# Gate weights: the low halves beside the high halves in one stationary tile

## What is computed

```python
x = x + 0.5 * _swiglu(_rmsnorm(x, ffn1_norm), ffn1_w_gate, ffn1_w_up, ffn1_w_down)
h = _rmsnorm(x, mix_norm)
p = h @ w_in                     # 1024 x 3080
bg, cg, xin, q, k, v, o, ip, fp = jnp.split(p, offs, axis=-1)
li = ip + b_igate                # 4 heads
lf = jax.nn.log_sigmoid(fp + b_fgate)   # 4 heads
```

## Time and profile before

| | |
|---|---|
| median of 3 runs | 2062.49 us (2058.13 to 2064.17) |
| the profiled execution | 2062.03 us |
| its span | 2060.1 us |
| TensorE busy (matmuls) | 2002.5 us, 97%, 12520 matmuls |
| VectorE busy | 910.5 us, 44% |
| ScalarE busy | 503.3 us, 24% |
| GpSimd busy | 91.5 us, 4% |
| mean granted TensorE clock | 0.99 |
| chain that ended last | TensorE 91%, VectorE 5% |

### The profile page before, as it was taken

The page is one execution under the profiler, slowest core; times in us unless marked ns, Lnnn a source line. Parts: engine busy times, 40 slices in busy tenths (PEclk is TensorE's granted clock), DMA queues, the critical chain, the costliest instruction groups (busy, mean ns, idle before and its releaser), DMA issues.

```text
span 2060.1 us, 31004 instructions
## 1 busy us (share of the span) xinstructions
PE 2002.5 (97%) x12520; PEld 1984.1 (96%) x12520; DVE 910.5 (44%) x1563; ACT 503.3 (24%) x896; POOL 91.5 (4%) x145
## 2 busy tenths in 40 slices
PE   6999999999999998999999889999999999999998
PEld 6999999999999998999999889999999999999998
DVE  6523433333333338522677737533333333333334
ACT  5302111121121124343444423221111211121122
POOL 1000000000000013200000011100000000000001
PEclk9999999999999999999999999999999999999999
DMA  6012101110111011211112230121011101110102
GB/s 208 21 42 61 61 20 41 61 61 20 41 61 61 11 42 65 75 50 33 32 31 80 68 86 21 41 62 61 20 41 61 61 20 41 61 61 20 51 1 85
DMA packets 144177, 105.09 MB, mean 51 GB/s; under 512 B 6376, under 2 KB 136248, under 8 KB 144120
## 3 DMA queue, kind: packets, MB, share of 16 engines
q1 hardware_dynamic: 143992, 104.26, 16.5%
q10 hardware_dynamic: 128, 0.03, 0.0%
HBM read 95.36 MB, written 8.92 MB: 51 GB/s over the span
## 4 chain that ended last, share of the span: by engine, by line
PE 91%; DVE 5%; ACT 1%; DMA 1%; issue 1%; SPq 1%; ACTq 0%; DVEq 0%; POOL 0%
PE bank L204 29%; PE bank L210 28%; PE bank L209 28%; PE bank L208 1%; PE bank L206 1%; DVE ffn_normed L171 1%; DVE in_lo L163 1%; DMA raw<-in_w_out 1%; DVE ffn_root_work L143 0%; PE bank L1975 0%; PE bank L637 0%; PE bank L1989 0%; PE bank L1988 0%; PE bank L861 0%; DMA vector_rows<-in_cache_conv 0%
## 5 line engine op out<-in xcount | busy, mean ns | idle before, releaser
L204 PE MATMUL bank<-in_hi,w_hi 128*128 128x352 f32 x2256 | 738.8, 327 | 16.5 <-DVE in_lo L1128 7.5
L210 PE MATMUL bank<-in_hi,w_lo 128*128 128x352 f32 x2256 | 728.8, 323 | 0.0
L209 PE MATMUL bank<-in_lo,w_hi 128*128 128x352 f32 x2256 | 727.2, 322 | 0.0
L204 PEld LDWEIGHTS bank<-in_hi,w_hi 128*128 128x128 f32 x2256 | 425.8, 189 | 21.6 <-DVE in_lo L1128 8.1
L209 PEld LDWEIGHTS bank<-in_lo,w_hi 128*128 128x128 f32 x2256 | 428.0, 190 | 1.1
L210 PEld LDWEIGHTS bank<-in_hi,w_lo 128*128 128x128 f32 x2256 | 426.2, 189 | 0.0
L394 DVE TENSOR_TENSOR ffn_hidden<-ffn_silu,bank 128x352 f32<-128x352 f32 x132 | 68.8, 521 | 669.4 <-PE bank L210 579.6
L204 PE MATMUL bank<-ffn_hidden_hi,ffn_w_hi_more 128*128 128x352 f32 x1056 | 342.2, 324 | 0.9 <-ACT ffn_hidden_hi L341 0.8
L405 DVE SCALAR_TENSOR_TENSOR x<-bank,x 128x352 f32<-128x352 f32 x528 | 267.3, 524 | 159.5 <-PE bank L210 111.2
L210 PE MATMUL bank<-ffn_hidden_hi,ffn_w_lo_more 128*128 128x352 f32 x924 | 297.9, 322 | 0.0
L209 PE MATMUL bank<-ffn_hidden_lo,ffn_w_hi_more 128*128 128x352 f32 x924 | 297.6, 322 | 0.0
(11 more groups left out here) (227 smaller groups left out, 1500.6 us busy)
## 6 DMA issues: line engine op xcount, KB each, us to landing
raw<-in_ffn_w_gate SPq DMA_DIRECT2D x44, 512.0 KB, 3.9
ffn_raw_more<-in_ffn_w_down SPq DMA_DIRECT2D x44, 512.0 KB, 5.5
raw<-in_w_in SPq DMA_DIRECT2D x24, 512.0 KB, 3.9
raw<-in_ffn_w_up SPq DMA_DIRECT2D x22, 512.0 KB, 5.0
ffn_raw_more<-in_ffn_w_up SPq DMA_DIRECT2D x22, 512.0 KB, 5.3
x_parked<-x SPq DMA_DIRECT2D x3, 1408.0 KB, 5.6
x<-x_parked SPq DMA_DIRECT2D x3, 1408.0 KB, 9.9
raw<-in_w_out SPq DMA_DIRECT2D x8, 512.0 KB, 4.0
```

The source lines that it names most:

```text
L204: pe.matmul(out, w_hi, in_hi, start=first, stop=False)
L209: pe.matmul(out, w_hi, in_lo, start=False, stop=False)
L210: return pe.matmul(out, w_lo, in_hi, start=False, stop=last)
```

## The change

The gates' tile uses 8 of 128 stationary columns. In it the low halves of the gate weights now stand in columns 64 to 67 and 96 to 99 of the *high* tile of slot 0, beside the high halves in 0 to 3 and 32 to 35. One matmul with the high input gives both the high and the low weights' products, and one with the low input as well. So each feature step of the gates has two matmuls instead of three, 48 instead of 72 over the three blocks (and the product of low weight with low input, which was left out, is now in). The two output groups land on partitions 0 and 32 (high) and 64 and 96 (low) of the same bank, and VectorE adds them: six copies out of the banks into the row `m_`, and two adds of 1056 tokens. The numbers of the steps after it, waited for by ScalarE, VectorE and TensorE, rise by two.

```diff
+    def gates_low(dve):
+        dve.wait_ge(m.w_high, 1)
+        halves = sh.w_hi[0].rearrange("p (k e n) -> p k e n", k=KT, e=2)
+        raw = sh.raw[0].rearrange("p (k e n) -> p k e n", k=KT, e=2)
+        dve.tensor_tensor(halves[:, :, 1, :], raw[:, :, 0, :], halves[:, :, 0, :].bitcast(FP32), ALU.subtract
+                          ).then_inc(m.w_low, 1)
+
     def early_low(dve):
-        low(dve, 0, 0)
+        gates_low(dve)
         low(dve, 1, 1)
...
             row = rows[0:HEADS, ROW_M, 0:TOKENS]
-            act.wait_ge(s.row_step, 3)
+            act.wait_ge(s.row_step, 5)
             act.activation(row, row, ACT.Exp, scale=-1.0).then_inc(s.row_exp, 1)
...
             for which, dst in ((0, a), (1, wk)):
                 part = slice(32 * which, 32 * which + HEADS)
+                low_part = slice(64 + 32 * which, 64 + 32 * which + HEADS)
                 for b in range(BLOCKS):
-                    last = dve.tensor_scalar(dst[:, block_columns(b)], first_banks[2][b][part, 0:BLK],
-                                             gate_bias[part, :], None, ALU.add)
+                    dve.tensor_scalar(dst[:, block_columns(b)], first_banks[2][b][part, 0:BLK],
+                                      gate_bias[part, :], None, ALU.add)
+                    last = dve.tensor_copy(m_[:, block_columns(b)], first_banks[2][b][low_part, 0:BLK])
                 row(last)
+                row(dve.tensor_tensor(dst, dst, m_, ALU.add))
             row(dve.scalar_tensor_tensor(m_, wk, -1.0, wk, ALU.mult, ALU.max))
             low(2, 3)
...
                 pe.wait_ge(m.w_low, 1)
-                product(b, 2, first_banks[2][b])
+                for k in range(KT):
+                    col = slice(k * P, (k + 1) * P)
+                    for half in (sh.in_hi, sh.in_lo):
+                        last = pe.matmul(first_banks[2][b][:, 0:BLK], sh.w_hi[0][:, col], half[:, k, block_columns(b)],
+                                         start=k == 0 and half is sh.in_hi, stop=k == KT - 1 and half is sh.in_lo)
+                last.then_inc(s.dense_done, 1)
                 pe.wait_ge(m.w_low, 2)
```

More of the change, by code:

```diff
@@ L1436, in _ @@
             act.wait_ge(s.constants, CONSTANTS)
-            act.wait_ge(s.row_step, 20)
+            act.wait_ge(s.row_step, 22)
             for dst, src, scale in ((row_inter[:, :], row_inter[:, :], 1.0),
@@ L1448, in _ @@
             for i, rest in enumerate(both):
-                act.wait_ge(s.row_step, 21 + i)
+                act.wait_ge(s.row_step, 23 + i)
                 act.activation(middle_rows[i], rest, ACT.Copy).then_inc(s.row_exp, 1)
@@ L1631, in _ @@
             row(dve.tensor_tensor(decay_row[:, :], max_before[:, :], max_last[:, :], ALU.subtract))
-            assert step == 20
+            assert step == 22
             low(2, 6)
@@ L1644, in _ @@
                 dve.wait_ge(s.row_exp, 9 + 2 * i)
-                dve.wait_ge(s.row_step, 21 + i)
+                dve.wait_ge(s.row_step, 23 + i)
                 dve.tensor_tensor(row_parts[64:64 + HEADS, i, :], rest, middle_rows[i].bitcast(FP32), ALU.subtract
@@ L2066, in mixer_phase @@
         sh.norm = next_norm
-ROW_STEPS = 24
+ROW_STEPS = 26
 def out_phase(nc, sh, o, f):
```

## The result

| | before | after |
|---|---|---|
| median of 8 runs | 2063.85 us (2058.13 to 2064.52) | 2069.39 us (2066.86 to 2071.61) |
| ratio | | 1.0033, 95% interval 1.0024 to 1.0042 |
| span of the profiled execution | 2060.1 us | 2066.6 us |
| TensorE matmuls | 12520 | 12496 |

What follows compares the result with a forecast made beforehand. TensorE bounds the kernel, VectorE the two gaps ahead of blocks 1 and 2. A fourth tile 3.7 us late plus 1.5 us of low clock gives 2062.03 + 5.2 = 2067.2 us, counted as no change; range 2062.5 to 2070.5.

Steps and rivals of the forecast that it cites:

- early low half: VectorE's norm chain before the blocks: 512 columns instead of 1024, 0.68 us long, letting the second start 0.19 us earlier.
- TensorE's bound and its two gaps: Ahead of blocks 1 and 2 TensorE waits for VectorE's norm: removed matmuls gain nothing, gaps grow to 3.2 and 2.55 us.
- The row chain: Gate rows on VectorE after block 2: six added copies, 3.16 us, and two adds, 2.58 us, together 5.74 us.
- blocking: The two new VectorE adds meet GpSimd's SBUF reads during the gate rows: 1.0 us, between 0 and 2.4.
- The stand and the start of the fourth tile: After block 2 TensorE stands 5.1 us for the fourth tile's low weight half and starts that tile 3.7 us later.
- The clock: Behind TensorE's 5.1 us wait after block 2 the granted clock falls: 1.5 us taken, bounds none to 3.0.
- slower rival: The clock also falls in the blocks, slowing block 2's 16 gate matmuls by 2.2 us: 2069.4 us, chance 0.34.
- The copy on ScalarE "costs nothing": ScalarE's bank copy behind exponential and logarithm moves 5.3 us to 846.7; TensorE needs the bank at 848.4: no cost.
- "Nothing absorbs the 5.2": Everything after the edited stage hangs on TensorE's order, even the late output-weight load, so the 5.2 us reaches the end.

Runs made afterwards that it cites:

- filler in the blocks: Changed kernel with eight more matmuls ahead of the gates' product in blocks 0 and 1 only, so these have 72 again; ratio 1.0029.
- rows alone: Changed kernel with its six copies and two adds, but the gates' three matmuls per feature step and the full early low half put back; ratio 1.0029.
- adds from the bank: Changed kernel with six adds of 4 x 352 reading the low group straight from the bank, replacing the copies and two long adds; ratio 1.0017.
- matmuls alone: Kernel before with only TensorE's part of the change, without the added VectorE copies and adds; ratio 0.9996.

## Why the prediction was wrong
I gave 2067.2 us and no change, with 0.34 for slower; it came out at 2069.4 and slower by 0.33%, just beyond the 0.3% that I had set as the border. The time lies 2.2 us over the forecast, but 1.4 of these come with the base: the median before is 2063.85 us over eight executions, 2062.49 over the first three. The stage is the cleaner comparison. My sum has 5.2 us; the stage measured 6.4, and the early low half gave back 0.2 ahead of it, so 6.2. Point by point:

- **TensorE's bound and its two gaps**: right. Blocks 0 and 1 gave nothing (filler in the blocks), the gaps grew.
- **The early low half**: 0.69 us, expected 0.68; the second came straight behind ScalarE. Right.
- **The row chain**: 5.74 + 1.0 us expected, 6.55 measured. The reads and copies took 0.56 each when they alternate, not 0.527, which is 0.4 us more over twelve; blocking took 0.4 instead of 1.0 us. The first add was not blocked here: it came first, and GpSimd's selection waited:

```profile
837.31 1.72 POOL L1360 TENSOR_SCALAR_AFFINE_SELECT x<-x 128x512 f32<-128x512 f32 x1
...
840.56 1.95 POOL L1373 CAST mix_row_parts<-x 128x2112 fp32r<-128x2112 f32 x1
```

  The selection takes 0.64 us otherwise; it was held by the add of 837.28. The second add, begun at 841.97, met the last 0.5 us of the cast and took 1.64 us. With the rows alone it was the first add that was held (1.62 us) and not the second. By the Trainium skill (SBUF — State Buffer, Who interferes with whom) the port pair that VectorE and GpSimd share is an exclusive lock, and the order of issue decides which of them waits. The traces agree: 1.72 for 0.64 us where the add came first, and 2.57 for 1.25 us where the cast did (adds from the bank).
- **The stand and the start of the fourth tile**: 5.1 us of standing and 3.7 us late expected; 5.1 (from the start of the last matmul to the start of the next) and 3.5 measured (3.7 in the stage, less the 0.2). The wait and its size are right, but the closeness is in part luck: the longer reads and the smaller blocking nearly cancelled, and blocking depends on how GpSimd's steps happen to lie.
- **The clock: the step that failed.** "I take 1.5, since part of the low stretch falls into the stand". It measured 2.7 us: the granted clock was 0.50 for all of 846.1 to 851.7, so the low clock began in the stand as I had said, and still lasted 5.6 us behind it. These 1.2 us are more than the 1.0 by which the sum was short. I had both prices in rows 10, 1.5 behind a gap of 2.7 us and 3.0 behind one of 3.2, and a stand of 5.1 us before me; the row nearest to it was the second. With 3.0 the sum is 6.7 us, and with the 2.7 measured 6.4, both beyond the border. The term varies, though: behind a stand as long, the fourth tile's first block took 2.8 us more than in the kernel before with the rows alone, and only 1.7 more with the filler in the blocks. The same 1.5 us more stand in my text as a way for the slower rival ("3.0 instead of 1.5 us behind the stand does the same"), so the mechanism was there and was priced at its cheaper end.
- **The rest of the slower rival**, a low clock in block 2: it was 1.00 there. Block 1 took the low clock and the gap behind it paid, as I had written against this rival.
- **The copy on ScalarE "costs nothing"**: true in the changed kernel, and only because the low half was later still. Its small slack, 1.7 us by my text, is the reason why moving the low halves gained nothing.
- **"Nothing absorbs the 5.2"**: not quite; the wait for the last output weights gave back 0.5 us (7.8 to 7.3).

## What to carry to other kernels
When matmuls are taken from a stage and work is put on an engine that feeds it, count from the new, earlier time at which TensorE asks, and list everything that queues behind the added work on each engine that waits for it: here two weight halves and, through ScalarE's exponential, a bank copy, with 1.3, 0.6 and 2.8 us of slack in the kernel before (the copy ended at 841.87 us and was needed at 840.9 + 3.8). A stand of several us costs itself and then the clock: price it by the row whose gap is nearest in length, and where rows differ, give both prices their chance. If the added work isn't urgent, put what TensorE needs ahead of it on every queue: done on VectorE alone it handed the wait on to ScalarE (1.0033), done on both it removed it (0.9991). ScalarE's order alone was not run.

## What the runs showed that I had not expected
- A VectorE step that gets earlier can get longer. Without the added rows, the step behind the logarithm came 1.3 us sooner, met GpSimd's cast and took 2.33 instead of 1.26 us; of the 1.3 us gained in the stage 0.5 were left.
- The clock's low stretch is part price, part cover: with it held up by filler matmuls, a second wait of 0.9 us came out from under it, and 2.7 us of slow matmuls were worth 1.4.
- The low clock can't be read off the length of the gap. Behind stands of about 5 us it lasted 5.6, 5.9 and once 3.4 us in three kernels. Behind the stand of 2.4 us of the adds from the bank the granted clock stayed at 1.00; in the kernel that also has both low halves moved up, the wait of 2.3 us inside the fourth tile was followed by 13 matmuls at a granted clock of 0.54:

```profile
846.30:850.00 3.70, 3.66 (x13) 0.54 0.06 9
```

- The same holds ahead of block 1. Nine kernels have the wider gap there, 3.6 to 3.7 us from one matmul's start to the next; in eight of them the clock fell to 0.50 behind it, in the ninth, the kernel with the matmuls alone, it stayed at 1.00. With the rows alone a gap of 2.5 us was followed by a low clock, where 2.3 us in the kernel before were not. None of this cost more than 0.2 us, as the gap behind block 1 paid for it.
